# Expert stage: every quarter of a block's weights goes through fixed buffers

## The reference, cut to what matters

```
def run_block(args):
    e, toks = args
    xb = x_pad[toks]
    h = jax.nn.silu(xb @ w1[e]) * (xb @ w3[e])
    return h @ w2[e]
...
y = yb.reshape(-1, D) * slot_gate[:, None]
return jnp.zeros((N + 1, D), x2.dtype).at[slot_tok].add(y)[:N]
```

## Time and profile before

| | us |
|---|---|
| median of 3 runs (lowest, highest) | 3585.07 (3575.14, 3587.28) |
| profiled execution | 3562.87 |
| its span | 3561.2 |
| expert stage of layer 0, from 679 to 1009 | 330 |
| expert stage of layer 1, from 1712 to 2030 | 318 |

### The profile page before, as it was taken

One profiled execution on the slowest core, in us unless ns is written; L12 is line 12 of the kernel. 1 busy time (PEld: TensorE's weight loads), 2 busy tenths in 40 slices (PEclk: granted clock), 3 DMA queues, 4 the chain that ended last, 5 costly groups with the idle time before them and its releaser, 6 DMA issues. The chain is left out here.

```text
span 3561.2 us, 66273 instructions
## 1 busy us (share of the span) xinstructions
PE 3308.4 (93%) x25798; PEld 1826.1 (51%) x25799; DVE 1330.2 (37%) x2441; ACT 896.6 (25%) x1525; POOL 341.2 (10%) x286
## 2 busy tenths in 40 slices
PE   8998999789979999999799889999999799999998
PEld 5445444567754444444677634443444477444443
DVE  1565111456542662112566530110348665410102
ACT  1125110356541143112456520000011522100000
POOL 1000000312230000002222220000000042000000
PEclk9999999899989999999899989999999999999999
DMA  7110323399632112223799412226212000122221
GB/s 266 60 59 34 109 78 134 152 383 411 265 127 71 60 36 97 81 72 141 288 413 396 155 61 71 82 76 154 72 70 71 23 2 3 71 82 71 82 79 62
DMA packets 80493, 447.10 MB, mean 126 GB/s; under 512 B 19904, under 2 KB 20040, under 8 KB 33488
## 3 DMA queue, kind: packets, MB, share of 16 engines
q1 hardware_dynamic: 52128, 377.51, 27.8%
q0 software_dynamic: 25280, 64.54, 5.6%
q10 hardware_dynamic: 2928, 3.07, 0.3%
HBM read 412.05 MB, written 32.89 MB: 125 GB/s over the span
## 5 line engine op out<-in xcount | busy, mean ns | idle before, releaser
L993 PE MATMUL pb<-arena,streamed 128*128 128x512 f32 x1408 | 608.5, 595 | 4.1 <-DVE arena L2037 3.3
L993 PEld LDWEIGHTS pb<-arena,streamed 128*128 128x128 f32 x1408 | 268.4, 191 | 343.5 <-issue 335.3
L892 PE MATMUL pb<-arena,xT 128*32 x3008 | 356.3, 277 | 51.6 <-issue 30.4
L647 PE MATMUL pb<-xT,streamed 128*128 128x512 f32 x832 | 367.8, 601 | 0.0
L892 PE MATMUL pb<-streamed,xT 128*32 128x128 f32 x9024 | 358.4, 277 | 3.6 <-issue 3.6
L892 PEld LDWEIGHTS pb<-arena,xT 128*32 128x32 f32 x3008 | 325.0, 112 | 69.4 <-issue 63.4
L818 PE MATMUL pb<-xT,streamed 128*128 128x512 f32 x768 | 335.4, 595 | 2.5 <-ACT arena L1410 2.5
L892 PEld LDWEIGHTS pb<-streamed,xT 128*32 128x32 f32 x9024 | 328.4, 112 | 4.2 <-issue 4.1
L1019 PE MATMUL pb<-arena,streamed 128*128 128x512 f32 x704 | 310.4, 604 | 11.3 <-DMA streamed<-in_w_tail 8.8
L1430 ACT ACTIVATE streamed<-arena 128x3072 f32 x94 | 260.2, 2768 | 58.0 <-SPq L419 40.2
L647 PEld LDWEIGHTS pb<-xT,streamed 128*128 128x128 f32 x832 | 159.4, 193 | 200.2 <-issue 200.0
(11 more groups left out here) (357 smaller groups left out, 3533.9 us busy)
## 6 DMA issues: line engine op xcount, KB each, us to landing
arena<-in_w_moe SPq DMA_DIRECT2D x192, 1024.0 KB, 11.6
streamed<-in_w_tail SPq DMA_DIRECT2D x87, 1024.0 KB, 4.8
streamed<-in_w_layer SPq DMA_DIRECT2D x78, 1024.0 KB, 4.8
xT<-xs_dram POOLq DMA_DIRECT2D x22, 512.0 KB, 8.6
ys_dram<-xT POOLq DMA_DIRECT2D x88, 128.0 KB, 9.1
xs_dram<-lnw POOLq DMA_DIRECT2D x12, 512.0 KB, 17.8
lnw<-in_ln_par POOLq DMA_DIRECT2D x4, 1024.0 KB, 5.6
rel_dram<-arena POOLq DMA_DIRECT2D x1, 4092.0 KB, 88.1
```

The source lines that it names most:

```text
L647: last = mm(pb[bank][:, 0:cols], unit(w, u, k), rhs[:, k * cols:(k + 1) * cols], start=(k == 0), stop=(k == KC - 1))
L892: last = mm(pb[m][r0:r0 + MOE_BLOCK, 0:FW], rows, w, start=(k == 0), stop=(k == KC - 1))
L993: last = mm(pb[3 * u + s][:], unit(w, u, k), xn[:, k * S:(k + 1) * S], start=(k == 0), stop=(k == KC - 1))
```

## The change

ScalarE and VectorE copy all four quarters of `w1`, `w3` and `w2`. `w1` goes to the first two slots of the ring in two copies, each with an increment of its own semaphore, and `up` waits for the second half at half of its steps. `w3` goes to the third slot of the ring and to the place of `memT`, in two copies. `w2` goes to a buffer for its first three row groups and two small ones for the fourth, in four copies. TensorE has no register addresses and no `slot` any more. SyncE gives a slot back when the last copy from it is done. Since `memT` is overwritten, SyncE loads it again at the end of layer 0, between the first and the second slot of the ring.

```diff
...
 FW, DW = D_EXP // COLS, D // COLS
-RELAY = KC * (D_EXP - FW)
-assert RELAY == 4 * (D - DW)
+HALF_K = KC // 2
+HALF_W = HALF_K * D_EXP
+W2_FIRST = 3
+assert HALF_W == PAIR
 G_POOL, G_Q, G_MQ, G_K, G_IQ, G_IK, G_V, G_IW, N_G = 0, 4, 8, 12, 16, 20, 21, 25, 26
...
         lnw = sb("lnw", NT * S)
+        w2_spare = sb("w2_spare", S)
         bias_p, bias_g = sb("bias_p", DEPTH * N_G), sb("bias_g", DEPTH * 24)
...
         sel, sel_b, last_sel, last_b, last_selT = (take(S) for _ in range(5))
-        w1_relay, w3_relay = streamed[:, 0:RELAY], streamed[:, RELAY:2 * RELAY]
-        w2_relay = sr[:, 13312 - S - RELAY:13312 - S]
+        w1_relay = [ring[0], ring[1]]
+        w3_relay = [ring[2], memT]
+        w2_relay = sr[:, 13312 - S - W2_FIRST * D:13312 - S]
+        w2_rest = [am[:, 3 * FW + D:3 * FW + D + S], w2_spare[:, :]]
         rat = [0]
         def rtile(cols):
             def copies_used(s, layers):
-                if s < 2:
+                if s == 1:
+                    sp.wait_ge(up_ready, 2 * layers * N_BLK + 2)
+                    if layers < DEPTH:
+                        sp.dma_start(memT, a["memT"]).then_inc(mem_loaded, 16)
+                elif s == 0:
                     sp.wait_ge(up_ready, 2 * layers * N_BLK + 1 + s)
...
                 for e in range(2, N_EXP):
-                    end = sp.value_load(blk_tab[0:1, 2 * N_BLK + e - 2:2 * N_BLK + e - 1], min_val=0, max_val=N_BLK)
+                    end = sp.value_load(blk_tab[0:1, 2 * N_BLK + e - 2:2 * N_BLK + e - 1], min_val=1, max_val=N_BLK)
                     for m in range(3):
                         arrived(e - 1, m)
-                        if m < 2:
-                            sp.wait_ge(up_ready, l * (2 * N_BLK) + 2 * end + 1 + m)
+                        if m == 0:
+                            sp.wait_ge(w1_relayed, l * (2 * N_BLK) + 2 * end)
                         else:
-                            sp.wait_ge(y_ready, l * N_BLK + end + 1)
+                            sp.wait_ge((w1_relayed, w3_relayed, w2_relayed)[m], l * N_BLK + end)
                         alone(sp)
...
             pe.sem_inc(dn_free, 2)
-            pe.wait_ge(mem_loaded, 16)
             for l in range(DEPTH):
                 def memory(l, groups):
+                    pe.wait_ge(mem_loaded, 16 * (l + 1))
                     for g in groups:
                         linear(pair(g // 2, l), g % 2, memT, l * LIN_LAYER + g, g % 2, N_MEM)
...
                     last.then_inc(xs_tr, 1)
-                def slot(b):
-
-                    return pe.value_load(blk_tab[0:1, b:b + 1] if isinstance(b, int) else blk_tab[0:1, bass.ds(b, 1)], min_val=0, max_val=SLOT)
-
-                def up(b, s, off, tile):
+                def up(b, s, tile):
                     pe.wait_ge(xsT_ready, l * N_TILE + tile + 1)
                     alone(pe)
-                    for m, (relay, relayed) in enumerate(((w1_relay, w1_relayed), (w3_relay, w3_relayed))):
-                        pe.wait_ge(relayed, l * N_BLK + b + 1)
-                        alone(pe)
+                    for m in range(2):
+                        if m:
+                            pe.wait_ge(w3_relayed, l * N_BLK + b + 1)
+                            alone(pe)
                         for k in range(KC):
+                            if m == 0 and k % HALF_K == 0:
+                                pe.wait_ge(w1_relayed, l * (2 * N_BLK) + 2 * b + 1 + k // HALF_K)
+                                alone(pe)
                             for g in range(COLS):
...
                                 rows = xsT[:, k * P + s % COLS * MOE_BLOCK:k * P + (s % COLS + 1) * MOE_BLOCK]
-                                w = arena[:, bass.ds(off + (m * KC + k) * D_EXP, FW)] if g == 0 else relay[:, (k * (COLS - 1) + g - 1) * FW:(k * (COLS - 1) + g) * FW]
+                                at = k % HALF_K * D_EXP + g * FW
+                                w = (w1_relay, w3_relay)[m][k // HALF_K][:, at:at + FW]
                                 last = mm(pb[m][r0:r0 + MOE_BLOCK, 0:FW], rows, w, start=(k == 0), stop=(k == KC - 1))
                         last.then_inc(up_ready, 1)
...
                     last.then_inc(ht_ready, 1)
-                def down(b, s, off):
+                def down(b, s):
                     pe.wait_ge(hT_ready, l * N_BLK + b + 1)
...
                             r0 = g * MOE_BLOCK
-                            w = arena[:, bass.ds(off + UP_PIECES * PAIR + k * S, DW)] if g == 0 else w2_relay[:, (k * (COLS - 1) + g - 1) * DW:(k * (COLS - 1) + g) * DW]
+                            w = w2_relay[:, k * D + g * DW:k * D + (g + 1) * DW] if k < W2_FIRST else w2_rest[g // 2][:, g % 2 * DW:(g % 2 + 1) * DW]
                             last = mm(pb[2 + s % 2][r0:r0 + MOE_BLOCK, 0:DW], hT[:, h0:h0 + MOE_BLOCK], w, start=(k == 0), stop=(k == 3))
                     last.then_inc(y_ready, 1)
...
                 alone(pe)
-                up(0, 0, slot(0), 0)
+                up(0, 0, 0)
                 pe.wait_ge(last_picked, l + 1)
...
                 with pe.Fori(0, N_TILE - 1) as i:
-                    off = slot(i * COLS)
                     for s in range(1, COLS + 1):
                         b = i * COLS + s
-                        ahead = slot(b)
-                        up(b, s, ahead, i + s // COLS)
+                        up(b, s, i + s // COLS)
                         if s == COLS - 1:
                             transpose_xs(i + 1)
-                        down(b - 1, s - 1, off)
+                        down(b - 1, s - 1)
                         turn(b)
-                        off = ahead
-                off = slot(N_BLK - 3)
                 for s in (1, 2):
                     b = N_BLK - 3 + s
-                    ahead = slot(b)
-                    up(b, s, ahead, N_TILE - 1)
-                    down(b - 1, s - 1, off)
+                    up(b, s, N_TILE - 1)
+                    down(b - 1, s - 1)
                     turn(b)
-                    off = ahead
-                down(N_BLK - 1, 2, off)
+                down(N_BLK - 1, 2)
                 def last_tile(t):
                     act.wait_ge(expert_here[0], l * N_EXP + e + 1)
                     alone(act)
-                    fn(cut(w1_relay, D_EXP - FW), cut(arena[:, bass.ds(slot_of(e), KC * D_EXP)], D_EXP)[:, :, FW:D_EXP], ACT.Copy).then_inc(w1_relayed, 1)
+                    for n in range(2):
+                        fn(w1_relay[n], arena[:, bass.ds(slot_of(e) + n * PAIR, PAIR)], ACT.Copy).then_inc(w1_relayed, 1)
                 def copy_xsT(j):
                     dve.wait_ge(expert_here[1], l * N_EXP + e + 1)
                     alone(dve)
-                    v.tensor_copy(cut(w3_relay, D_EXP - FW), cut(arena[:, bass.ds(slot_of(e) + 2 * PAIR, KC * D_EXP)], D_EXP)[:, :, FW:D_EXP]).then_inc(w3_relayed, 1)
+                    for n in range(2):
+                        last = v.tensor_copy(w3_relay[n], arena[:, bass.ds(slot_of(e) + (2 + n) * PAIR, PAIR)])
+                    last.then_inc(w3_relayed, 1)
                 dve.wait_ge(route_ready, l + 1)
...
                     dve.wait_ge(expert_here[2], l * N_EXP + e + 1)
                     alone(dve)
-                    src, out = slot_of(e) + UP_PIECES * PAIR, cut(w2_relay, D - DW)
                     for n in range(2):
-                        lo, hi = max(DW, n * S), (n + 1) * S
-                        if hi > lo:
-                            last = v.tensor_copy(out[:, :, lo - DW:hi - DW], cut(arena[:, bass.ds(src + n * PAIR, PAIR)], S)[:, :, lo - n * S:hi - n * S])
+                        at = slot_of(e) + (UP_PIECES + n) * PAIR
+                        v.tensor_copy(cut(w2_relay, D)[:, :, n * S:(n + 1) * S], cut(arena[:, bass.ds(at, W2_FIRST * S)], S))
+                        last = v.tensor_copy(w2_rest[n], arena[:, bass.ds(at + W2_FIRST * S, S)])
                     last.then_inc(w2_relayed, 1)
                 def hidden(b):
```

## The result

| | kernel before | changed kernel |
|---|---|---|
| median of the runs, us (lowest, highest) | 3586.14 (3575.14, 3587.28), 4 runs | 3625.23 (3619.24, 3628.54), 4 runs |
| profiled execution, us; its span | 3562.87; 3561.2 | 3623.38; 3621.6 |
| tile of four blocks, layer 1 | 24.97 | 27.36 |
| VectorE busy over the span, us | 1330.2 | 1590.5 |
| GpSimd busy over the span, us | 341.2 | 277.7 |

The ratio is 1.0112 (95%: 1.0092 to 1.0133): 1.1% slower, 39 us, where I had forecast no change. The profiled execution before (3562.87) is shorter than all four timed ones, so the whole times of these two profiles aren't compared with each other; a pair from one chip comes further down.

The account below looks back on a forecast made before the run. Weight DMA was taken to bound until expert 15 arrives, the engines afterwards. Layer 0 -3.2 +0.4 -0.5, border +3.8, layer 1 -3.3 +2.5 +0.5 -0.5: -0.3 us, median 3585; range 3577 to 3593, 8 in 10 3574 to 3602.

Parts of the forecast that it names:

- VectorE, the step that failed: VectorE's copies per block, priced at 0.53 ns an element and 0.15 us a copy: `w3` 2.36 us, `w2` 2.49 us.
- a rule that moved the sum by 0.7 us: VectorE fp32 copies lock the port pair shared with GpSimd; layer 1's last stores up to 0.7 us later, sum +0.4.
- The chain: Expert-stage tile of four blocks, followed start by start (kind is block number modulo 4): 25.22 us for 24.97, +0.25 a tile.
- `w1` and `w3`: Half-size copies of 2048 elements: 1.92 us for `w1` on ScalarE, 1.22 us for `w3` on VectorE.
- Address loads: TensorE's `slot` loads go, freeing 1.17 us ahead of each block numbered 1 modulo 4.
- Slots back at the copy: SyncE's earlier ring release brings expert weights sooner: layer 0 -3.2 us, layer 1 -3.3 us.
- the start of a layer: First blocks of a layer, longer first copies against an earlier block 1: +0.5 us in layer 1, bounds 0 and 1.
- memT: Reload at the end of layer 0 delays TensorE's start on `memT` by 3.8 us, nothing hiding it; bounds 2.6 and 6.
- B: Copies don't overlap, so `w2` is late for `down` at each block: +0.9 a tile, +11, 3596 us; chance 0.16.
- C: GpSimd's stores hold up VectorE's copies, 0.7 us each: +2.8 a tile, +33 us, 3618 us; chance 0.04.
- A: The copies hide and the tile goes to 23.80 us: -9, 3576 us; chance 0.17.
- D: The 1.17 us are the turn of the loop, not the loads: +1.3 a tile, total +15, 3600 us; chance 0.08.

Follow-up runs that it names:

- even copies: Changed kernel with each 1536-element `w2` copy written as 2 x 3 x 256 in place of 3 x 512; 3562.40 us beside 3565.70, ratio 0.9986.
- best: Changed kernel with 2 x 3 x 256 `w2` copies, gathers after the last block's `up`, next tile's `xsT` copied between the `w1` halves; 3556.20 us beside 3565.70, ratio 0.9976.
- with the loads put back: Changed kernel with 2 x 3 x 256 `w2` copies and the old `slot` loads back on TensorE, values unused; 3568.43 us beside 3560.55, ratio 1.0025.
- 3 x 256 twice: Changed kernel with each 3 x 512 `w2` copy written as two copies of 3 x 256; 3574.54 us beside 3560.55, ratio 1.0034.
- split three and one: Kernel before with each VectorE `w2` copy split by output rows into three rows, then one; 3576.26 us beside 3567.46, ratio 1.0032.
- two and two: Kernel before with each VectorE `w2` copy split by output rows into two rows and two; 3567.82 us, ratio 1.0005.

## Why the prediction was wrong

Four profiles of one chip, one execution each, cut at starts of `up` (block numbers) and ends of the last `down`; us:

| stretch | before | changed | even copies | best |
|---|---|---|---|---|
| start to block 0, layer 0 | 683.34 | 689.15 | 683.99 | 685.46 |
| blocks 0 to 38 | 265.26 | 271.79 | 258.36 | 260.06 |
| blocks 38 to 46 | 49.40 | 54.73 | 49.99 | 48.83 |
| block 46 to the end of `down` | 10.35 | 14.27 | 12.11 | 10.40 |
| to block 0, layer 1 | 705.77 | 706.10 | 706.52 | 706.24 |
| blocks 0 to 38 | 252.91 | 266.85 | 245.59 | 245.65 |
| blocks 38 to 46 | 51.78 | 54.71 | 53.60 | 55.58 |
| block 46 to the end of `down` | 13.03 | 14.30 | 11.67 | 10.40 |
| rest | 1531.51 | 1532.24 | 1531.59 | 1532.06 |

The changed kernel is 40.8 longer: 15.8 in layer 0's expert stage (the second to fourth line), 18.1 in layer 1's, and 5.8 ahead of the first block, where only the copies for block 0 are longer; there the profiles of all kernels here scatter between 681.8 and 690.2, so I put this down to no cause. The expert stages do repeat: 322.3 to 325.0 and 314.4 to 317.7 us in three profiles of the kernel before, 339.6 to 340.8 and 335.9 to 336.9 in the two of the changed kernel without the stall.

- **VectorE, the step that failed.** "2048 elements take 1.22 us and 3072 take 1.76: 0.53 ns an element" was carried over to 1536 elements of another shape: 0.95 forecast, 1.747 measured, `w2` of a block 4.07 in place of 2.49. Both rows that I took the rate from have an even number of rows; the new copy has three. The Trainium skill says it ("VectorE: DVE Perf Modes", section "Mode 2×_2P — use both read ports for one tensor"): the two ports take one half each of the outermost dimension, which must be "even (or odd and equal for src and dst)". By that rule, with which the traces here agree (1747, 1745 ns against 955), the copy runs at one element a cycle, and I should have weighed it instead of a rule that moved the sum by 0.7 us. That touching rows of a source count as one run is not on that page; it is my reading of the runs above.
- **The chain itself held.** Put 4.07 for 2.49 into it: `w2` done at 6.84 + 4.07 = 10.91, `down` at 11.21, kind 2 at 13.34; measured 11.05 and 13.17. With even copies, where the price of 0.95 is true, the forecast offsets and the measured ones are: kind 1 at 5.64 and 5.61, `down` at 9.63 and 9.61, kind 2 at 11.76 and 11.73, kind 3 at 17.5 and 17.36, the next tile at 25.22 and 25.01.
- **`w1` and `w3`.** 1.92 and 1.22 forecast, 1.906 and 1.226 measured.
- **Address loads.** 1.17 forecast at kind 1. With even copies it comes 1.25 us sooner (5.61 for 6.86), and 0.47 is lost ahead of kind 2 and 0.82 in the two steps to the next kind 0; put back, the loads cost 1.03 a tile.
- **Slots back at the copy.** Blocks 0 to 38 of layer 0 with even copies are 6.9 shorter than in the kernel before (4.2 against its first profile); forecast 3.2 less. In layer 1 blocks 0 to 38 are 7.3 shorter; I had 3.3 less, plus 2.5 and 0.5. Most of the extra lies in the first four blocks: 29.80 against 34.63 us. Block 1 starts 4.95 behind block 0 and not 6.63, and the third group of loads behind block 0 is issued at 15.7 and not 24.6 us; I had called the start of a layer a loss of 0.5. How much of this repeats is open: with the loads put back these four blocks took 33.92.
- **memT.** Forecast +3.8, "nothing hides it". The late `down` hid it: 0 to 0.4. TensorE gets there before the load only when it is early, for 0.75 to 3.19.
- **Rivals.** B had the sign and the mechanism (`w2` late for `down`, though at two blocks of four and not at each) but priced only lost seams; 27.36 lay beyond its end. With the right duration it would have been the forecast: 10 tiles of layer 1 at +2.4, less the 3.3 us of late arrivals, is +21, and the stage measured +18.1. C: the `w3` copies show no hold-up (1226 ns). A and D fell. A's terms as listed add up to -8.4 and not -9.
- **The range.** 3577 to 3593 was narrower than its own bounds: its tile of 23.80 to 25.9 in place of 25.22, over 11.75 tiles, is alone -16.7 to +8.0 us. And none of the bounds let a copy take longer than its priced 0.95 us.

## What to carry to other kernels

A VectorE copy's rate goes by its shape and not only by its size: before pricing a new copy by another one's ns per element, compare the outermost dimension of source and target, after runs that touch have been merged. Where it is odd on one side alone, reorder the same elements so that it is even. And when a change lengthens an engine's chain that has no slack left, the range must hold the case in which one of its new pieces costs twice.

## What the hardware showed besides

- Three rows on both sides cost what four rows do: 688 to 696 ns for 3 x 256, 694 for 4 x 256; 2 x 256 took 423 in its group. At the rate of the 1747 ns copy 3 x 256 would be 0.95 us.
- GpSimd's stores of `y` got twice as fast in the slower kernel. Their groups in the kernel before, then in the changed one:

```profile
L535 POOL DMA_DIRECT2D ys_dram<-xT x88 | 122.6, 1393 | 395.0 <-ACT xT L1465 385.3 <-issue 9.7
```

```profile
L544 POOL DMA_DIRECT2D ys_dram<-xT x88 | 62.5, 710 | 474.8 <-ACT xT L1470 461.7 <-issue 13.1
```

With even copies they take 1104 ns, with 3 x 256 twice 777, in the kernel before split three and one 702, two and two 1020. In the kernel before, the 27 stores that begin beside a 2048-element copy take 1163 ns in the mean and end 256 ns behind it; in the changed one, the 82 that begin beside the 1747 ns copy take 700. So in these two groups the copy at the fast rate holds up the store that meets it, and the slow copy doesn't. The Trainium skill's lock of the shared port pair ("SBUF — State Buffer", "SBUF: two separate sides") says the same of GpSimd's writes, and they agree. Not all stores do: 77 stores that begin beside a 3 x 256 copy take 748, though its rate is above that of the slow copy; why is open. The gathers wait 8.8 us for the last stores in both kernels, so the shorter ones moved no time.
- It goes the other way too, once the copies are even-shaped: the 512-element `w2` copies that overlap a store take 565 ns at the median, the others 414. That is rival C's mechanism, at 0.15 us for such a copy.
